# One ScalarE gelu in place of five steps on two engines, and two convolutions moved two places later on VectorE, in a two-layer hybrid decoder kernel

## The reference, cut to what matters

```python
p = h @ ev_w_in[j]
y_a = _rwkv7_time_mix(p[..., :RWKV_COLS], ...)
y_b = _rglru_block(xb=p[..., RWKV_COLS:RWKV_COLS + LRU_WIDTH], gb=p[..., RWKV_COLS + LRU_WIDTH:], ...)
mix = jnp.concatenate([y_a, y_b], axis=-1) @ ev_w_out[j]

def _rglru_block(xb, gb, conv_w, conv_b, wa, ba, wx, bx, lam):
    xb = _causal_dwconv(xb, conv_w, conv_b)                 # 4 taps, 512 channels
    gate_r = sigmoid(blockdiag(xb, wa) + ba)
    gate_i = sigmoid(blockdiag(xb, wx) + bx)
    log_a = -8.0 * softplus(-lam) * gate_r
    u = sqrt(-expm1(2.0 * log_a)) * (gate_i * xb)
    h = associative_scan(exp(log_a), u)
    return h * gelu(gb)                                     # the tanh form of gelu
```

## Time and profile before

| | us |
|---|---|
| median of three runs | 1858.58 |
| lowest and highest of them | 1857.56, 1860.25 |
| the profiled execution, its own time | 1857.38 |
| its span in the profile | 1855.4 |

### The profile page before, as it was taken

One profiled execution on the slowest core, in us unless ns is written; L12 is line 12 of the kernel. 1 busy time (PEld: TensorE's weight loads), 2 busy tenths in 40 slices (PEclk: granted clock), 3 DMA queues, 4 the chain that ended last, 5 costly groups with the idle time before them and its releaser, 6 DMA issues.

```text
span 1855.4 us, 26637 instructions
## 1 busy us (share of the span) xinstructions
PE 1690.4 (91%) x10910; PEld 1394.4 (75%) x10910; DVE 1119.1 (60%) x1357; ACT 749.6 (40%) x999; POOL 215.2 (12%) x189
## 2 busy tenths in 40 slices
PE   7996998899899999999995877789898999999996
PEld 6775897788778888888784655568887778888885
DVE  3689464563675543434669987885656665434345
ACT  4552542353444232323544464643545252323231
POOL 5112310000000000000026633420000000000000
PEclk9997999999899999999998898799998999999999
DMA  5220002353023233323221221003441223332331
GB/s 189 76 69 23 4 4 93 126 153 109 21 92 103 92 101 95 99 95 120 80 80 46 69 68 68 1 12 125 122 140 35 91 80 102 91 102 91 103 125 57
DMA packets 40872, 155.52 MB, mean 84 GB/s; under 512 B 4528, under 2 KB 4656, under 8 KB 39600
## 3 DMA queue, kind: packets, MB, share of 16 engines
q1 hardware_dynamic: 40752, 153.83, 25.9%
HBM read 151.72 MB, written 2.10 MB: 83 GB/s over the span
## 4 chain that ended last, share of the span: by engine, by line
PE 72%; DVE 21%; ACT 4%; issue 3%; DMA 0%; SPq 0%; POOL 0%; DVEq 0%; ACTq 0%; POOLq 0%
PE bank L548 21%; PE bank L549 21%; PE bank L550 21%; DVE cacc L1594 4%; DVE w_lo L1578 3%; DVE sconv L1594 1%; DVE p L1591 1%; DVE h L1594 1%; PE bank L710 1%; DVE nbh L1639 1%; DVE act_lo L1591 1%; PE bank L723 1%; PE bank L676 1%; PE bank L729 1%; ACT w_hi L1113 1%
## 5 line engine op out<-in xcount | busy, mean ns | idle before, releaser
L1578 DVE TENSOR_TENSOR w_lo<-w_raw,w_hi 128x1024 fp32r<-128x1024 f32 x263 | 335.2, 1275 | 294.0 <-ACT w_hi L1113 291.5
L548 PE MATMUL bank<-act_lo,w_hi 128*128 128x512 f32 x1048 | 421.3, 402 | 53.9 <-DVE w_lo L1578 45.3
L1113 ACT ACTIVATE w_hi<-w_raw 128x1024 fp32r<-128x1024 f32 x263 | 279.0, 1061 | 355.4 <-PE bank L550 343.2
L549 PE MATMUL bank<-act_hi,w_lo 128*128 128x512 f32 x1048 | 416.8, 398 | 0.0
L550 PE MATMUL bank<-act_hi,w_hi 128*128 128x512 f32 x1048 | 416.2, 397 | 0.0
L548 PEld LDWEIGHTS bank<-act_lo,w_hi 128*128 128x128 f32 x1048 | 202.6, 193 | 105.8 <-issue 48.6
L550 PEld LDWEIGHTS bank<-act_hi,w_hi 128*128 128x128 f32 x1048 | 202.2, 193 | 43.3
L549 PEld LDWEIGHTS bank<-act_hi,w_lo 128*128 128x128 f32 x1048 | 202.6, 193 | 42.4 <-issue 0.7
L548 PE MATMUL bank<-w_lo,aux_hi 128*128 128x512 f32 x576 | 224.5, 390 | 5.3 <-DVE act_lo L1591 5.3
L549 PE MATMUL bank<-w_hi,aux_lo 128*128 128x512 f32 x576 | 224.1, 389 | 0.0
L550 PE MATMUL bank<-w_hi,aux_hi 128*128 128x512 f32 x576 | 224.1, 389 | 0.0
(11 more groups left out here) (355 smaller groups left out, 2234.2 us busy)
## 6 DMA issues: line engine op xcount, KB each, us to landing
w_raw<-weights SPq DMA_DIRECT2D x263, 512.0 KB, 3.6
gb<-ln_rows SPq DMA_DIRECT2D x6, 1024.0 KB, 5.8
stage<-x_feat SPq DMA_DIRECT2D x4, 512.0 KB, 6.0
h<-x_tok SPq DMA_DIRECT2D x1, 2048.0 KB, 8.8
stage<-mem_feat SPq DMA_DIRECT2D x2, 1024.0 KB, 5.8
out<-h SPq DMA_DIRECT2D x4, 512.0 KB, 2.6
lora_sb<-lora SPq DMA_DIRECT2D x1, 512.0 KB, 8.6
lru_sb<-lru_w SPq DMA_DIRECT2D x1, 512.0 KB, 9.4
```

Of the source, the lines that this page charges most:

```text
L548: pe.matmul(o, whi, xlo, start=first, stop=False)
L549: pe.matmul(o, wlo, xhi, start=False, stop=False)
L1113: act.activation(w_hi[:, s], w_raw[:, s], ACT.Copy).then_inc(S("w_hi_done"), 1)
L1578: dve.tensor_tensor(w_lo[:, s], w_raw[:, s], f(w_hi[:, s]), ALU.subtract).then_inc(S("w_split"), 1)
```

## The change

Gelu of the four gate tiles becomes one ACTIVATE with the function Gelu_apprx_tanh, in place on `p0`. The square, the tanh and the four POOL instructions go, with the semaphore `l_gact`, and `l_gelu` counts to 1 instead of 4. POOL's clears of `yt_(0, 1)` and `yt_(1, 1)` used to stand behind the first two gelu steps; they now wait for `chunk_done` 22. ACT no longer waits for POOL ahead of the recurrence's sigmoids. On DVE, `convolution(2)` and `convolution(3)` stand behind `masked_products(0)` and `bonus(1)` instead of ahead of both.

```diff
@@ POOL
-            pool.wait_ge(S("l_gact"), 1)
-            gelu(pool.tensor_scalar(li[:], li[:], 0.044715, 1.0, ALU.mult, ALU.add))
-            gelu(pool.tensor_tensor(li[:], li[:], g_, ALU.mult))
+            pool.wait_ge(S("chunk_done"), 22)
             clear(yt_(0, 1), 0)
             clear(yt_(1, 1), 0)
             pool.wait_ge(*made("rprod", 10))
             clear(yt_(0, 2), 0)
-            pool.wait_ge(S("l_gact"), 2)
-            gelu(pool.tensor_scalar(li[:], li[:], 1.0, 0.5, ALU.add, ALU.mult))
-            gelu(pool.tensor_tensor(g_, g_, li[:], ALU.mult))
@@ ACT
                 if i == 21:
-                    done(act.activation(li[:], p0[:, 18:22, PAD:PW], ACT.Square), "l_gact")
+                    g_ = p0[:, 18:22, PAD:PW]
+                    done(act.activation(g_, g_, ACT.Gelu_apprx_tanh), "l_gelu")
@@ ACT
             tokens(0)
-            act.wait_ge(S("l_gelu"), 2)
-            done(act.activation(li[:], li[:], ACT.Tanh, scale=0.7978845608028654), "l_gact")
             tokens(1)
@@ ACT
-            act.wait_ge(S("l_gelu"), 4)
@@ DVE
             split(FIRST["out0"] + W_SLOTS)
-            for j in range(2, 4):
-                dve.wait_ge(S("in_out"), 15 + j)
-                convolution(j)
             masked_products(0)
             bonus(1)
+            for j in range(2, 4):
+                dve.wait_ge(S("in_out"), 15 + j)
+                convolution(j)
             masked_products(1)
@@ DVE, lru_scan(0)
-                    dve.wait_ge(S("l_gelu"), 4)
+                    dve.wait_ge(S("l_gelu"), 1)
```

## The result

| | before | after |
|---|---|---|
| median, us | 1858.16 (4 runs) | 1848.8 (4 runs) |
| lowest and highest | 1857.56, 1860.25 | 1847.84, 1849.46 |
| the profiled execution: time, span | 1857.38, 1855.4 | 1849.46, 1847.5 |

The ratio is 0.9947, with a 95% interval of 0.993 to 0.9964, so the change saves 9.4 us by the medians. The forecast was 1849.1.

The account below looks back on a forecast made before the run. PE was taken as waiting 17.06 us for VectorE's first copy of m, then running slowly; -5.7 - 5.9 + 2.15 = -9.45 us took 1857.38 to 1847.9, and with the median 1.2 higher, 1849.1; range 1845.2 to 1853.2.

Parts of the forecast that it names:

- POOL held up VectorE for 5.7 us: Ahead of the first copy of m, POOL's gelu steps lengthen nbh by 1.56 us and w_lo by 4.17 us.
- The convolutions' 5.88 us ahead of the first copy: Moving two convolutions off VectorE's path to the first copy of m saves 5.88 us; PE's gap shrinks to 5.5 us.
- The clock after the gap: PE's clock falls to half in its first gap and returns 8 us after work resumes, as before.
- The cost in the second half: Convolutions ahead of masked_products(1) make PE wait 1.1 us at its fifth set and delay the pak products; cost 2.15 us.
- the second rival: PE's new wait in the second half costs clock, up to 4 us at half clock: 1853.1 us; chance 0.1.
- The sum: Over the changed stage: -5.7 - 5.9 + 2.15 = -9.45 us.
- Gelu and its loads at nothing: On ACT, the second new 1.28 us load ahead of the sigmoids is covered by one us of slack.
- The slower rival: Clock falls in PE's first new gap and small products do not lift it; 1867 us if lasting 18 us; chance 0.03.

Follow-up runs that it names:

- e1: The changed kernel with the two convolutions back ahead of the first reads, so only the gelu part of the change; 1852.25 us, ratio 0.997 to before.
- e3: The kernel before with POOL's first two gelu steps replaced by clears of the same buffer, which read nothing; 1852.8 us, ratio 0.9977 to before.
- e2: The kernel before with only the two convolutions moved, gelu staying on POOL; 1861.2 us, ratio 1.0025 to before.
- e5: The changed kernel with PE's last 32 products ahead of its first gap done seven times; 1847.67 us, ratio 0.9947 to before.
- e10: e6 with PE's wait ahead of the levels filled by its last lru product, done seven times; 1853.31 us, ratio 0.998 to before.
- e4: The changed kernel with the two convolutions between masked_products(0) and bonus(1); 1846.56 us, ratio 0.994 to before.
- e7: The changed kernel with the convolutions behind masked_products(1) and lru waiting for them one by one; 1845.41 us, ratio 0.994 to before.
- e12: The changed kernel with one more table load and tiny activation on ScalarE ahead of the recurrence's sigmoids; 1848.17 us, ratio 0.9953 to before.
- e11: The changed kernel with two more table loads and tiny activations on ScalarE ahead of the recurrence's sigmoids; 1892.7 us, ratio 1.0192 to before.
- e6: The changed kernel with four more table loads and tiny activations on ScalarE ahead of the recurrence's sigmoids; 1897.05 us, ratio 1.0215 to before.

## Why the prediction was right, point by point

- **POOL held up VectorE for 5.7 us.** Right, and the cause is shown: e1 takes POOL's steps away and both operations fall to 1.23 us; e3 keeps POOL busy without reading and they do too; e2 brings the same delay about in another place, 5.76 us. The prediction names the multiply alone, but `nbh` ran beside the one-input step before it (line 472, to 154.69).
- **The convolutions' 5.88 us ahead of the first copy.** Right: the fifth set comes 11.86 us after S instead of 23.53, 11.67 us earlier for the 11.6 of the sum, and the gap is 5.39 us for 5.5.
- **The clock after the gap.** Taken as 8 us from resuming; it was 6.7 us. The second half's products start 26.08 us after S instead of 38.35 (187.69 in the timeline of PE), which is 12.3 us earlier for 11.6. The term was sized 0.7 us too low. That it came no further out is luck: with the same work behind the gap the clock was back 4.9 us (e1) to 8.0 us (before) after PE had resumed, and no row of the kernel before tells which.
- **The cost in the second half.** Computed as 2.15 us with a wait of PE of 1.1 us; the wait is 1.06 us, and the products with `pak` come 16.41 us after the second half's start instead of 13.76, a cost of 2.65 us, 0.5 more. About half of that is the short fall of the clock from 186.4 to 189.8, the second rival in small: e5 and e10 have the same wait without that fall and need 16.14 and 16.13 us. So the wait alone does not bring the fall about, and these runs do not show what decides. Where the other 0.3 us come from no run separates. e4 and e7, at 13.76 and 13.75 us, have the whole cost back.
- **The sum.** 9.45 us forecast, 9.62 us in the stage, 9.4 us by the medians. The two terms that were off, 0.7 and 0.5 us, had opposite signs and nearly cancelled; that the sum is closer than its terms is luck.
- **Gelu and its loads at nothing.** Right, with 1.0 us of slack as worked out. The price given if the cover were gone, "up to 1.3 us", prices a wait by its own length where PE's next 50 us are small products, and that does not hold in general: 0.48 us cost no more than itself (e12), 2.00 us cost 44 us (e11). What 1.3 us would have cost is not shown.
- **The slower rival.** Its mechanism is real, but it did not come from the gap in which I had put it: there the clock was back over the transposes, at 169.4, and so it was after the short fall of the second half, at 189.8. It waits at the levels, which the new load had brought within a microsecond. Its chance of 0.03 was too low for how thin that slack was.
- **Separate parts.** The prediction added the two edits as if each stood alone. e2 shows that the move without the new gelu is a loss, since the convolutions would then meet POOL's last two steps. The sum was right because both were made.

## What to carry to other kernels

An engine off the path can hold up one that is on it without any semaphore: look for operations longer than their neighbours of the same shape, and for what another engine reads in those microseconds. Before an instruction is moved, see what runs beside its new place, not only who waits for it. And where TensorE goes from full-size products into a long stretch of small ones, a wait ahead of that stretch is not priced by its length; keep the last microseconds ahead of it free of gaps, or fill them.

## What the runs showed of the hardware that I had not expected

The small products of the levels keep a clock of 1.00 once it is there (e10 and the kernel before, for some 50 us), but do not bring it back from 0.50: in e6 and e11 PE was busy all the time for 95 us and more at half clock. In both the clock came back only behind the levels, after PE had turned from their 64x32 products to the 64x64 products of line 741: at 304.9 in e6, 2.5 us after the first of them, and at 301.6 in e11, 4.5 us after. After PE's first gap, with 64x64 products and then 128x128 transposes, it was back within 4.9 to 8.0 us in all eleven kernels that have one without filling. What tells these stretches apart inside the chip, these runs do not show. The fall in e11 came 2.5 us after PE had resumed, so a stretch that begins at full clock is no sign that the wait before it was harmless.
